# A shorter warm-up matmul, TensorE's tail transposes and expert counts at other places, the root table earlier, two endings behind a branch

## The chip, the cores and the metric

The kernel runs on one core of a Trainium2 chip. The metric is the device time of one execution in microseconds (us); lower is better. TensorE (PE) multiplies, VectorE (DVE) and ScalarE (ACT) do the elementwise work, GpSimd (POOL) a little of it, and SyncE (SP) issues most of the transfers.

## The reference

One step of a decoder layer for 320 tokens (256 of a prompt, 64 of eight sequences) of width 1024: a mixer, then a mixture of 32 experts, then a last norm.

```python
h = rmsnorm(x, norm_mix_w); proj = h @ w_in            # 1024 x 3584
y_conv = bg * short_conv(cg * v_c, ...)                # 512 channels
o, new_hgrn = hgrn2_chunked(q, logf, k, i, state)      # 4 heads, 128 x 128 states
x = x + concat(y_conv, norm(o) * gnorm_w * silu(g)) @ w_out
t = rmsnorm(x, norm_ffn_w)
vals, idx = top_k(t @ router_w + router_b, 4); gates = softmax(vals)
for e in range(32):                                    # w_*[e]: 1024 x 1024 float32
    a = minimum(t @ w_gate[e] + b_gate[e], 7); u = clip(t @ w_up[e] + b_up[e], -7, 7)
    y += combine[:, e] * (((u + 1) * a * sigmoid(1.702 * a)) @ w_down[e] + b_down[e])
y_out = rmsnorm(x + y, final_norm_w)                   # and the new states
```

The 96 expert matrices are 4 MiB each, 403 MB together, and each is read once.

## The kernel before

**Phases.** The input projection and the HGRN2 levels run first (to about 157 us of the trace), then the output projection `wout` with the router beside it (to about 197 us), then the first expert's tokens are gathered and the 32 experts run one after the other.

**An expert.** At most 64 tokens (slots) go to an expert in a round. TensorE gathers their rows from three bf16 parts of the normed rows (`gather`, L1535 and L1538), turns the last expert's hidden rows and this one's tokens (`turn_hidden` L1697, `turn` L1625), turns the selection (`turn_gates`, L1600, L1609), and then does the last expert's down product, this one's gate product, the scatter of the last expert's result (L1639) and the up product. Each product is `product`, 16 float32 matmuls in the code of L1679, which the trace shows as 32 (x32), behind two short ones for the bias (L1654). An expert thus takes three products, and its down product stands in the next expert's turn.

**Loops.** Experts 0 and 1 are written out. The other 30 are a hardware loop (`pe.Fori(0, LOOPS)`, L1734) of six passes with five experts each; the other engines have the same loop. A pass of TensorE's loop is 1627 instructions: 550 matmuls in the code, which are 790 weight loads and 790 matmuls in the engine's stream, and 47 waits, register instructions and the branch. In that stream a bf16 matmul or a transpose is two instructions and a float32 product's matmul is four. Counted in the built program, 3228 instructions of TensorE stand before the loop's first one.

**Weights.** SP issues each matrix as one 4 MiB transfer into a ring of five places. Matrix i is issued when product i-5 has read its place (`wUsed`). The matrices at both ends come in halves and quarters, so that a product can begin with a part. They are numbered 3e for gate, 3e+1 for up, 3e+2 for down; number 93 is the gate matrix of expert 31.

**Further rounds.** `further_rounds` (L311 to L326) reads the number of rounds and branches. With one round, as here, each engine runs `ending` in the branch's first part and then jumps over the code of the further rounds; that code is long on TensorE (some 2300 instructions).

**Start and end.** Before the inputs are there, TensorE runs nine matmuls of 512 columns on a constant tile (`keep_busy`, L1244). `tails` (L1419) are four transposes of the last convolution rows, which ACT copies out (L668) and sends. `counts` (L1500) are three matmuls that count the tokens of each expert. At the end ACT scales the last down product (`yLast`, L759), loads the table of the square root (L651), and `norms` squares the three blocks (L769); for the third block TensorE's `fold_final` adds two halves (L1255), from which ACT's root, DVE's reciprocal and product and the last transfers follow. SP's `outputs` sends the results.

Of the kernel before, what the change touches and what calls it, by code (L numbers as in the profile page):

```python
# [5 lines left out]
def hybrid_shortconv_hgrn2_moe_step(nc, A):  # L6
# [91 lines left out]
    LG_BANK, PART_BANK = 5, 6  # L98
    POS_BANK, COUNT_AT = [5, 5, 6], 384
# [10 lines left out]
    with ctx:  # L110
# [48 lines left out]
        tailT = view(R1, 3328, shape=(512,))  # L159
# [94 lines left out]
        h2Parts, roundsDone, epsOut, maskOut = (sem("h2_parts"), sem("rounds_done"), sem("eps_out"),  # L254
# [4 lines left out]
        finScale, fnwIn, ptLastOut = sem("fin_scale"), sem("fnw_in"), sem("pt_last_out")  # L259
        x2Kept, accSet, combDone = sem("x2_kept"), sem("acc_set"), sem("comb_done")  # L260
# [5 lines left out]
        busyOut = sem("busy_out")  # L266
# [68 lines left out]
        def _(sp):  # L335
# [140 lines left out]
            further_rounds(sp, all_loads, ending=outputs)  # L476
# [47 lines left out]
        def _(act):  # L524
# [3 lines left out]
            act.wait_ge(epsOut, 1)  # L528
# [101 lines left out]
            def root2(b):  # L630
                if b < 2:
                    act.wait_ge(ssq2Done, b + 1)
                    total = st[:, 9 + b:10 + b]
                else:
                    act.wait_ge(foldMM, 2)
                    total = ps[:, PART_BANK, 0:1]
                act.activation(st[:, 12 + b:13 + b], total, ACT.Sqrt, bias=epsT[:], scale=1.0 / D).then_inc(root2Done, 1)
# [46 lines left out]
            root2(2)  # L684
            def one_round(r):
# [71 lines left out]
                act.activation(PTLast[:], slots_of(E - 1), ACT.Copy).then_inc(ptLastOut, 1)  # L757
                act.wait_ge(wUsed, (r + 1) * (LPE * E) + START)
# [3 lines left out]
            def norms():  # L762

                bring_table(ACT.Sqrt, 3)
# [26 lines left out]
        def _(dve):  # L791
# [14 lines left out]
            did(dve.memset(epsT[:], EPS), epsOut)  # L806
            dve.memset(busy, 1.0).then_inc(busyOut, 1)
# [178 lines left out]
            X2T_BANK = [6, 7]  # L986
# [35 lines left out]
            def remainder(b, p):  # L1022

                hf = h2f[:, b % 2, 0:WIDE[b]]
                dve.wait_ge(partDone, 2 * b + 1 + p)
                if p == 0:
                    dve.wait_ge(normed, b + 1)
                    TT(hf, hf, h2p[0][b], ALU.subtract).then_inc(resid, 1)
                else:
                    dve.wait_ge(resid, b + 1)  # L1030
                    if b:
                        dve.wait_ge(tailOut, 32)
                    TT(h2p[2][b], hf, h2p[1][b], ALU.subtract).then_inc(h2Parts, 1)

            def choose(b):

                dve.wait_ge(lgMM, b + 1)
                need(did(STT(lg[:, b, :], ps[:, LG_BANK, E * b:E * b + E], st[:, 15 + b:16 + b], rb[:], ALU.mult, ALU.add)))
# [19 lines left out]
            def place(b):  # L1058
# [3 lines left out]
                need(did(STT(posm[:, b, 0:E], ps[:, POS_BANK[b], 128 + E * b:128 + E * b + E], 1.0, sel[:, b, :], ALU.add, ALU.mult), posOut))  # L1062
# [51 lines left out]
            def one_round(r):  # L1114
# [59 lines left out]
                if isinstance(r, int):  # L1174
                    gate_parts(slice(0, 1)).then_inc(combDone, 1)
                    dve.wait_ge(roundsDone, 1)
                    rounds.append(count_of_rounds(dve))
# [60 lines left out]
        def _(pe):  # L1238
# [7 lines left out]
            pe.wait_ge(busyOut, 1)  # L1246
            keep_busy(9)
# [189 lines left out]
            def turn_x2(b):  # L1437
                if b == 2:
                    pe.wait_ge(x2TOut, 2)
                    for half in range(2):  # L1440
                        pe.wait_ge(x2Done, 3 + half)
                        for c in range(2 * half, 2 * half + 2):
                            ins = TR(ps[:, 6 + half, 128 * c:128 * c + 128], xb[2][:, 128 * c:128 * c + 128], ident)
# [20 lines left out]
            def sum_logits(b):  # L1464
# [3 lines left out]
                pe.wait_ge(*((selDone, b) if b else (tailTOut, 1)))  # L1468
                MM(ps[:, LG_BANK, E * b:E * b + E], lgPart, fours[:], start=True, stop=True).then_inc(lgMM, 1)

            def logits(half):
# [3 lines left out]
                pe.wait_ge(posOut, 2)  # L1475
# [6 lines left out]
            def positions(b):  # L1482
# [5 lines left out]
                for at in range(0, 128, n):  # L1488
                    ins = MM(ps[at:at + n, POS_BANK[b], 128 + E * b:128 + E * b + E], trib[0:n, 0:n], sel[0:n, b, :], start=(b == 0), stop=True)
                ins.then_inc(posMM, 1)  # L1490

            def earlier_blocks(b):

                for a in range(b):
                    MM(ps[:, POS_BANK[b], 128 + E * b:128 + E * b + E], onesb[:], sel[:, a, :], start=(a == 0), stop=False)

            def counts():

                for a, (_, na) in enumerate(TOK):
# [48 lines left out]
            tails()  # L1548
# [26 lines left out]
            counts()  # L1575
# [3 lines left out]
            def one_round(r):  # L1579
# [14 lines left out]
                def turn_gates(e, m):  # L1594
# [3 lines left out]
                    pe.wait_ge(uDone, e + START)  # L1598
                    for b, (t0, n) in enumerate(TOK):
# [163 lines left out]
            further_rounds(pe, one_round, close_round, ending=fold_final)  # L1763
# [44 lines left out]
```

## Time and profile before

| | us |
|---|---|
| median of 3 runs | 1145.14 |
| lowest, highest | 1144.82, 1148.22 |
| profiled execution, its own time | 1145.91 |
| its span, first to last instruction | 1144.1 |
| TensorE busy | 1098.0 (96%) |
| VectorE busy | 285.6 (25%) |
| ScalarE busy | 174.4 (15%) |
| mean granted TensorE clock | 0.98 |
| read from HBM | 428.26 MB, 378 GB/s over the span with what is written |

How to read the rows further down: in the chain of waits each row is a start, a length and what the chain ran through; "issue" is time for which the profile shows no cause. A time of a view counts from the start of the span. "PEldq" is the sequencer that feeds TensorE, "SPq" that of SyncE; a branch that it takes has a duration there. A row of the transfers' view gives the line, how many were issued in the window, their size, and the median time from issue to landing.

### The profile page before, as it was taken

The page shows a single profiled execution, that of the slowest core. Times are in us where ns is not written, and L with a number is a line of the kernel's source. Part 1 is how long each engine was busy: PE and PEld are TensorE (multiplying, and loading weights), DVE is VectorE, ACT ScalarE, POOL GpSimd, SP SyncE. Part 2 cuts the span into 40 slices and gives each one's busy share as a digit, 9 for nine tenths or more (in the row PEclk, how much of TensorE's full clock was granted, in tenths as well). Part 3 has the DMA queues.
Part 4 walks back from the last instruction along what each step waited for, and adds up shares of the span by engine and source line. Part 5 has one row for each costly group of instructions (what it writes and reads, how often), then busy time and mean ns, then how long its engine had stood idle before and what let it go on. Part 6 is the DMA issues. An engine that isn't in the chain of part 4 may idle for free.

```text
span 1144.1 us, 15330 instructions
## 1 busy us (share of the span) xinstructions
PE 1098.0 (96%) x6369; PEld 465.1 (41%) x6370; DVE 285.6 (25%) x609; ACT 174.4 (15%) x354; POOL 18.2 (2%) x45
## 2 busy tenths in 40 slices
PE   8999999999999799998999989999899999899996
PEld 5667754433333333333333323333333333333332
DVE  3165464411222111111222111222111111122211
ACT  4100124211111011111111101111111111111112
POOL 0002000000000000000000000000000000000000
PEclk9999999999999899999999998999989999899999
DMA  9971259999999999999999999999999999999961
GB/s 321 333 217 45 103 199 396 377 426 434 414 432 432 428 409 432 432 428 432 416 434 428 432 432 417 435 427 434 426 420 428 434 431 428 423 428 427 426 277 48
DMA packets 43076, 433.17 MB, mean 379 GB/s; under 512 B 3999, under 2 KB 23251, under 8 KB 26869
## 3 DMA queue, kind: packets, MB, share of 16 engines
q1 hardware_dynamic: 42112, 431.03, 90.8%
q8 instruction: 66, 1.08, 0.4%
q10 hardware_dynamic: 885, 0.95, 0.2%
q14 instruction: 13, 0.11, 0.0%
HBM read 428.26 MB, written 3.71 MB: 378 GB/s over the span
## 4 chain that ended last, share of the span: by engine, by line
PE 94%; issue 3%; DMA 1%; DVE 1%; ACT 1%; ACTq 0%; DVEq 0%
PE ps L1679 58%; PE ps L1306 9%; PE ps L1639 6%; PE ps L1535 4%; PE ps L1431 3%; PE ps L1654 3%; PE ps L1538 2%; PE ps L1625 2%; PE ps L1697 2%; PE ps L1296 1%; PE ps L1600 1%; PE ps L1609 1%; DMA ring<-in_w_in 1%; PE ps L1334 0%; DMA x<-in_x_prompt 0%
## 5 line engine op out<-in xcount | busy, mean ns | idle before, releaser
L1679 PE MATMUL ps<-ring,RT 128*64 128x512 f32 x2040 | 448.6, 592 | 0.0
L1679 PEld LDWEIGHTS ps<-ring,RT 128*64 128x64 f32 x2040 | 144.0, 137 | 271.4 <-issue 265.7
L1679 PE MATMUL ps<-ring,R 128*64 128x512 f32 x1024 | 229.4, 601 | 0.0
L1679 PEld LDWEIGHTS ps<-ring,R 128*64 128x64 f32 x1024 | 73.1, 140 | 135.8 <-issue 133.7
L1306 PE MATMUL ps<-R,ring 128*128 128x320 f32 x384 | 107.4, 436 | 0.8 <-DMA ring<-in_w_in 0.8
L1306 PEld LDWEIGHTS ps<-R,ring 128*128 128x128 f32 x384 | 71.7, 190 | 32.2 <-issue 2.7
L1191 DVE TENSOR_SCALAR RT<-ps 128x512 f32<-128x512 f32 x32 | 22.1, 692 | 227.3 <-PE ps L1679 227.3
L1141 DVE SCALAR_TENSOR_TENSOR RT<-ps,R 128x512 f32<-128x512 f32 x31 | 23.3, 751 | 220.7 <-ACT R L720 220.7
L693 ACT ACTIVATE RT<-ps 128x512 f32<-128x512 f32 x31 | 18.5, 597 | 345.4 <-PE ps L1538 345.4
L1639 PE MATMUL ps<-R 64*128 64x512 bf16 x558 | 69.3, 380 | 0.0
L1535 PE MATMUL ps<-R,P 128*64 128x512 bf16 x372 | 50.7, 409 | 13.0 <-issue 13.0
L1182 DVE TENSOR_SCALAR RT<-ps 128x512 f32<-128x512 f32 x32 | 22.1, 692 | 131.3 <-PE ps L1679 130.6
L720 ACT ACTIVATE R<-ps,R 128x512 bf16<-128x512 f32 x31 | 21.3, 687 | 208.1 <-PE ps L1679 208.1
L710 ACT ACTIVATE RT<-RT 128x512 f32<-128x512 f32 x32 | 20.2, 630 | 179.2 <-DVE RT L1182 179.2
L1132 DVE TENSOR_TENSOR RT<-ps,par 128x512 f32<-128x512 f32 x31 | 21.4, 692 | 100.9 <-PE ps L1625 100.9
L1639 PEld LDWEIGHTS ps<-R 64*128 64x128 bf16 x558 | 23.3, 98 | 56.3 <-issue 38.3
L1538 PE MATMUL ps<-R,P 128*64 128x256 bf16 x372 | 30.8, 288 | 15.1 <-issue 15.1
L1535 PEld LDWEIGHTS ps<-R,P 128*64 128x64 bf16 x372 | 22.2, 112 | 47.5 <-issue 34.8
L1654 PE MATMUL ps<-R,eh 128*64 128x512 bf16 x192 | 40.1, 414 | 0.9 <-ACT R L715 0.7
L1538 PEld LDWEIGHTS ps<-R,P 128*64 128x64 bf16 x372 | 23.3, 113 | 25.2 <-issue 18.6
L1185 DVE TENSOR_TENSOR RT<-RT 128x512 f32<-128x512 f32 x32 | 22.2, 693 | 24.5 <-ACT RT L710 24.5
L1625 PE MATMUL ps<-consts,RT 128*128 128x128 f32 x128 | 25.8, 329 | 1.4 <-ACT RT L693 0.5
(254 smaller groups left out, 603.0 us busy)
## 6 DMA issues: line engine op xcount, KB each, us to landing
ring<-in_w_up SPq DMA_DIRECT2D x25, 4096.0 KB, 17.6
ring<-in_w_down SPq DMA_DIRECT2D x25, 4096.0 KB, 20.2
ring<-in_w_gate SPq DMA_DIRECT2D x24, 4096.0 KB, 20.5
ring<-in_w_up SPq DMA_DIRECT2D x12, 2048.0 KB, 14.9
ring<-in_w_gate SPq DMA_DIRECT2D x12, 2048.0 KB, 18.1
ring<-in_w_down SPq DMA_DIRECT2D x10, 2048.0 KB, 16.3
ring<-in_w_in SPq DMA_DIRECT2D x14, 1024.0 KB, 11.9
ring<-in_w_down SPq DMA_DIRECT2D x8, 1024.0 KB, 16.6
```

What stands on the lines that cost most here:

```text
L1141: STT(yrest, ps[:, DOWN_BANK, :], gsl[:, buf(j):buf(j) + 1], ysb[0], ALU.mult, ALU.subtract).then_inc(yRest, 1)
L1182: TS(ga, ps[:, GATE_BANK, :], LIMIT, None, ALU.min).then_inc(aDone, 1)
L1185: TT(gt, ga, gs, ALU.mult).then_inc(tDone, 1)
L1306: ins = MM(ps[:, n % 2, 0:NT], slot_k(L, 256)[:, k, 128 * half:128 * half + 128], hT[:, k, :], start=(k == 0), stop=(k == KT - 1))
L1431: ins = MM(dst, mixT[k][:, t0:t0 + n], w[:, 512 * half:512 * half + 512], start=(k == 0), stop=(k == KT - 1))
L1535: ins = MM(in_fours(to), P[:, b, 0:SLOTS], half_of(h2p[part][b], half), start=(b == 0 and part == 0), stop=False)
L1538: ins = MM(in_fours(to[:, 256 * at:256 * at + 256]), P[:, 2 + at, 0:SLOTS], half_of(h2p[part][2], half), start=False, stop=(part == 2 and ...
L1625: ins = TR(ps[:, to, 128 * c:128 * c + 128], fourth(xgs, c), ident)
L1639: ins = MM(acc_rows(b, half), slots_of(j)[64 * half:64 * half + 64, t0:t0 + n], ysb[part][64 * half:64 * half + 64, :], start=False, stop= ...
L1654: MM(shape(ps[64 * half:64 * half + 64, to, :]), eh[:, par, :], cols(bias3[:, mat, :], half), start=True, stop=False)
L1679: ins = MM(shape(ps[64 * half:64 * half + 64, to, :]), lhs(k), cols(w, half), start=False, stop=(n == KT - 1))
L1697: ins = TR(ps[:, DOWN_BANK, 128 * c:128 * c + 128], fourth(hid, c), ident)
```

## The change

It does these things, and nothing else:

- The nine warm-up matmuls become 43 of 32 columns and 5 of 512 columns; the two signals `epsOut` and `busyOut` become one, `fillOut`.
- `tails` stands behind the whole of `wout` instead of after its first block, writes another bank (6 instead of 5), and ACT copies and sends it after the third block's root instead of after the first's, from another place in memory. DVE's wait for that transfer moves behind the counting of rounds. The transposed third block goes to banks 5 and 7 instead of 6 and 7, with waits that fit.
- `counts` stands in the first expert's `turn_gates` instead of ahead of `gather_first(1)`.
- ACT loads the square root's table ahead of its wait for the last down product instead of after `yLast`.
- SP's `outputs` and TensorE's `fold_final` are no longer written in both parts of the branch but once, behind it. ACT's and DVE's endings stay in it.

By count, 3309 instructions of TensorE stand before its loop: 39 more matmuls of two instructions and three more waits, 81 in all. The loop itself keeps its 1627.

```diff
@@ further_rounds of SP and of TensorE
-            further_rounds(sp, all_loads, ending=outputs)
+            further_rounds(sp, all_loads)
+            outputs()
...
-            further_rounds(pe, one_round, close_round, ending=fold_final)
+            further_rounds(pe, one_round, close_round)
+            fold_final()
@@ ACT
             root2(0)
-            act.wait_ge(tailMM, 1)
-            act.activation(tailT[0:18, :], ps[0:18, LG_BANK, :], ACT.Copy).then_inc(tailTOut, 1)
             keep_x2(0)
-            act.wait_ge(tailTOut, 1)
-            act.dma_start(A["new_conv_prompt"][0, 0], tailT[0:2, :]).then_inc(tailOut, 16)
-            act.dma_start(A["new_conv_sample"][0].rearrange("b w c -> (b w) c"), tailT[2:18, :]).then_inc(tailOut, 16)
...
             root2(2)
+            act.wait_ge(tailMM, 1)
+            act.activation(tailT[0:18, :], ps[0:18, TAIL_BANK, :], ACT.Copy).then_inc(tailTOut, 1)
+            act.wait_ge(tailTOut, 1)
+            act.dma_start(A["new_conv_prompt"][0, 0], tailT[0:2, :]).then_inc(tailOut, 16)
+            act.dma_start(A["new_conv_sample"][0].rearrange("b w c -> (b w) c"), tailT[2:18, :]).then_inc(tailOut, 16)
...
                 act.activation(PTLast[:], slots_of(E - 1), ACT.Copy).then_inc(ptLastOut, 1)
+                bring_table(ACT.Sqrt, 3)
                 act.wait_ge(wUsed, (r + 1) * (LPE * E) + START)
                 act.activation(yLast, ps[:, DOWN_BANK, :], ACT.Copy, scale=gsl[:, buf(E - 1):buf(E - 1) + 1]).then_inc(yHigh, 1)
...
             def norms():
 
-                bring_table(ACT.Sqrt, 3)
@@ TensorE
-            pe.wait_ge(busyOut, 1)
-            keep_busy(9)
+            def keep_busy_in_bits(n):
+
+                for _ in range(n):
+                    MM(ps[0:32, 1, 0:32], busy[:, 0:32], busy[:, 0:32], start=True, stop=True)
+
+            pe.wait_ge(fillOut, 2)
+            keep_busy_in_bits(43)
+            keep_busy(5)
...
             def tails():
                 pe.wait_ge(tailIn, 1)
+                pe.wait_ge(lgPartOut, 2)
                 for c in range(4):
-                    ins = TR(ps[0:18, LG_BANK, 128 * c:128 * c + 128], tail[:, c, :], ident)
+                    ins = TR(ps[0:18, TAIL_BANK, 128 * c:128 * c + 128], tail[:, c, :], ident)
...
             def counts():
 
+                pe.wait_ge(posOut, 3)
...
             pe.wait_ge(stSOut, NH)
-            tails()
             wout(1, range(KT // 2))
...
             wout(2, range(7, KT))
+            tails()
             turn_x2(2)
             logits(0)
             pe.wait_ge(ssq2Done, 3)
-            sum_halves(st[:, 11:12], ps[:, PART_BANK, 0:1]).then_inc(foldMM, 1)
+            pe.wait_ge(x2TOut, 4)
+            sum_halves(st[:, 11:12], ps[:, FOLD_BANK, 0:1]).then_inc(foldMM, 1)
             logits(1)
             pe.wait_ge(earlyP, 1)
             pe.wait_ge(h2Parts, 2)
+            pe.wait_ge(root2Done, 3)
             gather_first(0)
-            pe.wait_ge(root2Done, 3)
+            pe.wait_ge(lgRead, 3)
             earlier_blocks(2)
             positions(2)
-            counts()
             gather_first(1)
...
                     pe.wait_ge(uDone, e + START)
+                    if isinstance(r, int) and e is e0:
+                        counts()
```

TensorE at the very start of the program, with the change (the warm-up and what follows it):

```order
L1249 MATMUL ps<-RT 32x32 x43
L1244 MATMUL ps<-RT 128x512 x5
L1256 MATMUL ps<-consts,parRows 128x52
L1267 MATMUL ps<-consts,R 128x128 x8
L1261 MATMUL ps<-st,fold 64x1 x2
```

Before, one row of nine matmuls (L1244, 128x512 x9) stood ahead of the transpose of `parRows`; 48 matmuls stand there now.

TensorE from the last piece of `wout` (128x512 product, L1431) to the first expert's first transposes, before:

```order
L1431 MATMUL ps<-ring 64x512 x2
L1443 MATMUL ps<-consts,x 128x128 x4
L1478 MATMUL ps<-rw,R1 64x32 x8
L1255 MATMUL ps<-st,fold 64x1 x2
L1478 MATMUL ps<-rw,R1 64x32 x8
L1514 MATMUL ps<-R1,P 64x256 x12
L1495 MATMUL ps<-sel,onesb 128x32 x2
L1489 MATMUL ps<-sel,trib 64x32 x2
L1500 MATMUL ps<-sel,onesb 128x32 x3
L1514 MATMUL ps<-R1,P 64x256 x12
L1522 MATMUL ps<-x,R1 64x256 x4
L1600 MATMUL ps<-identb,P 128x128 x2
```

The same place with the change (lines are some eight to twelve higher):

```order
L1438 MATMUL ps<-ring 64x512 x2
L1426 MATMUL ps<-consts,tail 18x128 x4
L1451 MATMUL ps<-consts,x 128x128 x4
L1486 MATMUL ps<-rw,R1 64x32 x8
L1261 MATMUL ps<-st,fold 64x1 x2
L1486 MATMUL ps<-rw,R1 64x32 x8
L1523 MATMUL ps<-R1,P 64x256 x12
L1503 MATMUL ps<-sel,onesb 128x32 x2
L1497 MATMUL ps<-sel,trib 64x32 x2
L1523 MATMUL ps<-R1,P 64x256 x12
L1531 MATMUL ps<-x,R1 64x256 x4
L1509 MATMUL ps<-sel,onesb 128x32 x3
```

The four tail transposes now stand between `wout` and the third block's transposes, and the three counting matmuls behind the gathers.

TensorE's end in the program, with the change (before, `fold_final`'s two matmuls, L1255, stood between the last two rows):

```order
L1691 MATMUL ps<-ring,R1 64x512 x16
L1756 MATMUL ps<-RT,PTLast 128x512 x4
L1756 MATMUL ps<-RT,PTLast 64x512 x2
L311 TENSOR_LOAD rounds
L311 ISA x2
L316 COMPARE_AND_BRANCH
L316 UNCONDITIONAL_BRANCH
```

The jump over the further rounds (the last row) came after `fold_final` and comes ahead of it now.

## Rows read from the trace of the kernel before

**Rows 1.** Chain of waits, around the loop's second return: start us, us, what

```profile
525.59 6.87 PE ps L1679 x32
532.46 2.96 issue
535.41 2.54 PE ps L1535 x12
538.75 2.38 issue
561.98 6.87 PE ps L1679 x32
589.64 6.87 PE ps L1679 x32
```

**Rows 2.** Who waited for whom, TensorE: total us, times, longest us

```profile
PE ps L1538 <- issue: 15.1, 5, 4.5
PE ps L1535 <- issue: 13.0, 5, 3.0
```

**Rows 3.** Branches of TensorE's sequencer: count, ns min/median/max, when

```profile
L1734 PEldq COMPARE_BRANCH  x6: 83/6552/6927, 380.7 to 1117.1; - x6
L1734 PEldq COMPARE_BRANCH  x1: 6927/6927/6927, 528.1 to 528.1; - x1
L316 PEldq COMPARE_BRANCH  x2: 87/2386/4686, 1133.6 to 1137.7; - x2
```

**Rows 4.** Instruction queue: packets, MB, share; the page, 532 to 548 us, 541.2 to 673 us

```profile
q8 instruction: 66, 1.08, 0.4%
...
q8 instruction: 3, 0.05, 1.3%
...
q8 instruction: 6, 0.10, 0.3%
```

**Rows 5.** Stretches: us, PE, PEld, DVE, ACT, POOL busy (x), clock, DMA share, GB/s

```profile
400.00:410.00 10.00, 10.00 (x50) 3.30 (x48) 1.44 (x2) 1.32 (x2) 0.00 (x0) 1.00 0.93 372
535.40:538.75 3.35, 3.34 (x18) 1.76 (x18) 0.00 (x0) 0.00 (x0) 0.00 (x0) 0.55 1.06 455
562.00:679.00 117.00, 116.92 (x664) 44.31 (x660) 22.83 (x44) 14.93 (x32) 0.95 (x4) 1.00 1.00 430
```

**Rows 6.** Transfers, matrix 93: SP's issues, then second half's landing time, then its product

```profile
1062.82 3.76 SPq L348 DMA_DIRECT2D ring<-in_w_gate  x2
...
ring<-in_w_gate SPq DMA_DIRECT2D x1, 2048.0 KB, 21.8
...
1105.08 7.03 PE L1679 MATMUL ps<-ring,RT 128*64 128x512 f32 x32
```

**Rows 7.** Chain of waits, 160 to 206 us

```profile
170.82 0.44 PE ps L1419 x4
...
196.62 0.43 DVE x L993
...
200.57 0.27 PE ps L1500 x3
```

**Rows 8.** Timeline of the end: start, us, engine, line, what

```profile
1132.69 2.99 PE L1744 MATMUL ps<-RT,PTLast 64*128 64x512 f32 x12 [0.88 <-ACT RT L759]
1132.81 1.28 ACT L651 ACT_TABLE_LOAD   x1 [0.26 <-issue]
...
1134.21 1.01 ACT L769 ACTIVATE R<-ps 128x1024 f32<-128x1024 f32 x1
...
1137.68 0.28 PE L1255 MATMUL ps<-st,fold 128*64 128x1 f32 x4 [2.00 <-ACT R L769]
...
1139.50 0.56 ACTq L778 DMA_DIRECT2D y_sample<-R  x1
```

**Rows 9.** Timeline of the start

```profile
1.94 4.02 PE L1244 MATMUL ps<-RT 128*128 128x512 bf16 x9 [1.94 <-DVE RT L807]
...
6.31 0.34 PE L1250 MATMUL ps<-consts,parRows 52*128 52x52 f32 x1 [0.34 <-DMA consts<-in_consts]
```

More of the change, by code:

```diff
@@ L97, in hybrid_shortconv_hgrn2_moe_step @@
     UP_BANK, GATE_BANK, DOWN_BANK = 5, 6, 7
-    LG_BANK, PART_BANK = 5, 6
-    POS_BANK, COUNT_AT = [5, 5, 6], 384
+    LG_BANK, PART_BANK, TAIL_BANK, FOLD_BANK = 5, 6, 6, 7
+    POS_BANK, COUNT_AT = 5, 384
     FIRST_BANK = (4, 7)
@@ L158, in hybrid_shortconv_hgrn2_moe_step @@
         stP = view(RT, 0, "p (h d) -> p h d", shape=(4, 128), h=4)
-        tailT = view(R1, 3328, shape=(512,))
+        tailT = view(RT, 512, shape=(512,))
         x2T = view(R1, 3840, "p (k t) -> p k t", shape=(8, 128), k=8)
@@ L259, in hybrid_shortconv_hgrn2_moe_step @@
         finScale, fnwIn, ptLastOut = sem("fin_scale"), sem("fnw_in"), sem("pt_last_out")
+        lgRead = sem("lg_read")
         x2Kept, accSet, combDone = sem("x2_kept"), sem("acc_set"), sem("comb_done")
@@ L805, in _ @@
             TT, TS, STT = dve.tensor_tensor, dve.tensor_scalar, dve.scalar_tensor_tensor
-            did(dve.memset(epsT[:], EPS), epsOut)
-            dve.memset(busy, 1.0).then_inc(busyOut, 1)
+            did(dve.memset(epsT[:], EPS), fillOut)
+            dve.memset(busy, 1.0).then_inc(fillOut, 1)
             did(dve.memset(u[:, :, 0:2], 0.0))
@@ L985, in _ @@
             WB = [0, 2, 4]
-            X2T_BANK = [6, 7]
+            X2T_BANK = [5, 7]
             def add_mixer(b):
@@ L1037, in choose @@
                 dve.wait_ge(lgMM, b + 1)
-                need(did(STT(lg[:, b, :], ps[:, LG_BANK, E * b:E * b + E], st[:, 15 + b:16 + b], rb[:], ALU.mult, ALU.add)))
+                need(did(STT(lg[:, b, :], ps[:, LG_BANK, E * b:E * b + E], st[:, 15 + b:16 + b], rb[:], ALU.mult, ALU.add), lgRead))
                 need(did(dve.max(mx[:, b, :], lg[:, b, :])))
@@ L1061, in place @@
                 dve.wait_ge(selDone, b + 1)
-                need(did(STT(posm[:, b, 0:E], ps[:, POS_BANK[b], 128 + E * b:128 + E * b + E], 1.0, sel[:, b, :], ALU.add, ALU.mult), posOut))
+                need(did(STT(posm[:, b, 0:E], ps[:, POS_BANK, 128 + E * b:128 + E * b + E], 1.0, sel[:, b, :], ALU.add, ALU.mult), posOut))
                 if b == 2:
@@ L1175, in one_round @@
                     gate_parts(slice(0, 1)).then_inc(combDone, 1)
+                    dve.wait_ge(tailOut, 32)
                     dve.wait_ge(roundsDone, 1)
@@ L1439, in turn_x2 @@
                     pe.wait_ge(x2TOut, 2)
+                    pe.wait_ge(posOut, 2)
                     for half in range(2):
@@ L1442, in turn_x2 @@
                         for c in range(2 * half, 2 * half + 2):
-                            ins = TR(ps[:, 6 + half, 128 * c:128 * c + 128], xb[2][:, 128 * c:128 * c + 128], ident)
+                            ins = TR(ps[:, 5 + 2 * half, 128 * c:128 * c + 128], xb[2][:, 128 * c:128 * c + 128], ident)
                         ins.then_inc(x2TMM, 1)
@@ L1467, in sum_logits @@
                 pe.wait_ge(foldOut, 2)
-                pe.wait_ge(*((selDone, b) if b else (tailTOut, 1)))
+                if b:
+                    pe.wait_ge(selDone, b)
                 MM(ps[:, LG_BANK, E * b:E * b + E], lgPart, fours[:], start=True, stop=True).then_inc(lgMM, 1)
@@ L1474, in logits @@
                 pe.wait_ge(rwOut, 1)
-                pe.wait_ge(posOut, 2)
                 for k in ((0, 1, 4, 5), (2, 3, 6, 7))[half]:
@@ L1488, in positions @@
                 for at in range(0, 128, n):
-                    ins = MM(ps[at:at + n, POS_BANK[b], 128 + E * b:128 + E * b + E], trib[0:n, 0:n], sel[0:n, b, :], start=(b == 0), stop=True)
+                    ins = MM(ps[at:at + n, POS_BANK, 128 + E * b:128 + E * b + E], trib[0:n, 0:n], sel[0:n, b, :], start=(b == 0), stop=True)
                 ins.then_inc(posMM, 1)
@@ L1494, in earlier_blocks @@
                 for a in range(b):
-                    MM(ps[:, POS_BANK[b], 128 + E * b:128 + E * b + E], onesb[:], sel[:, a, :], start=(a == 0), stop=False)
+                    MM(ps[:, POS_BANK, 128 + E * b:128 + E * b + E], onesb[:], sel[:, a, :], start=(a == 0), stop=False)
             def counts():
+                pe.wait_ge(posOut, 3)
                 for a, (_, na) in enumerate(TOK):
```

9 lines of the change are left out of this document (3 added, 6 removed).

## The prediction

> **What bounds the kernel now.** I read the chain of waits first: it is TensorE nearly throughout, so I looked for the time in which TensorE does nothing. Within the loop an expert takes 27.66 us, from one up product to the next (561.98 to 589.64, [rows 1]). Across the loop's return the same stretch takes 36.39 us (525.59 to 561.98). So this return costs 8.73 us beyond the work, and there are five returns.
>
> Where these go: TensorE stops twice, 2.96 us right at the return and 2.38 us after the first 18 matmuls of the new pass [rows 1]. "Issue" means that no other engine and no weight transfer is behind it. Both gaps come once per return: 13.0 and 15.1 us over five, 28.1 together, or 5.6 each [rows 2]. The other 3.1 us of this return are work at half clock: the granted clock is 0.55 of full between the gaps [rows 5], a mixture of the 2.4 and 1.2 GHz levels, and the first 12 matmuls of 535.41 take 2.54 us. In the steady stretch it is 1.00.
>
> The cause is in the sequencer. The loop's branch takes 0.08 us where it falls through and up to 6.93 us where it is taken [rows 3]. In the 16 us around the return three packets of 16 KB come on the instruction queue, and only six in the next 132 us [rows 4]. Code comes in pieces. In the steady stretch 1324 weight loads and matmuls take 117 us [rows 5] and a piece is used up in about 132 / 6 = 22 us [rows 4], so a piece holds about 249 of them, which with the waits and register instructions among them (47 in 1627) makes 256. One piece lands after the jump. It holds only the first 36 weight loads and matmuls (18 matmuls) with their waits, some 40 instructions, and then TensorE waits again, for the next piece. So a piece's edge lies about 40 instructions behind the loop's first one.
>
> The second limit is not in TensorE's rows. The transfer engines are busy 1.00 of the steady stretch and move 430 GB/s [rows 5]. An expert's three matrices are 12.58 MB: 29.2 us at that rate, longer than the 27.66 us that TensorE needs. With the returns, five experts take TensorE 5 x 27.66 + 8.7 = 147 us, against 146 us for their weights. Today the two limits stand side by side.
>
> **The loop's code, 81 instructions later.** The edge that was 40 behind the loop's first instruction comes to lie 41 ahead of it, and the next is 256 - 41 = 215 behind it. This does three things.
> - The second gap goes. A piece of 215 instructions lasts some 15 us, and a fetch took about 2.5 us where it was waited for. Even if it were only asked for at the edge, the sequencer runs ahead of TensorE: it reached the branch at 528.1 [rows 3], 4.3 us before the product ended at 532.46 [rows 1], so at most some 0.5 us would show.
> - The jump gets shorter. Today the branch is 1627 - 40 - 6 x 256 = 51 instructions behind an edge, so, as I read it, the piece that comes after the loop has just been asked for, and the jump's own fetch waits for it: 6.93 us. The jump at the program's end, with nothing under way, takes 4.69 us [rows 3]. With the change the branch stands 132 instructions (some 11 us) behind an edge, and I take 4.69 us. Less the 4.3 us that the sequencer is ahead, and some 0.35 us to restart, the gap is 0.7 us.
> - With gaps of 0.7 us I expect the clock to stay at 2.4 GHz, as in the steady stretch.
>
> A return then costs 0.7 to 1.5 us instead of 8.7; I take 0.7, and TensorE alone would gain 5 x 8.0 = 40 us.
>
> The Trainium skill (Runtime: NRT & Kernel Launch, Instruction fetch mechanics) says that code comes in 16 KiB blocks of 256 instructions with the next block fetched ahead, and that a taken branch outside the window waits for a fetch; by that the trace agrees. The same section gives TensorE room for 2048 instructions. By that the loop of 1627 would stay inside and the shift would gain nothing. The six and three packets per pass [rows 4] speak against it.
>
> **What the weights let through.** 40 us is more than the weights allow. Their transfers run without a pause, so a faster TensorE doesn't bring them earlier. The closest place near the end is the gate matrix of expert 31 (number 93). Its second half is issued at about 1066.2, lands 21.8 us later at 1088.0, and is needed by the fifth of eight k-tiles of a product that starts at 1105.1, so at 1108.5 [rows 6]: 20.5 us of room, 20.3 with a semaphore's time. All that follows it on TensorE (23 us) stays as it is. TensorE will then wait for weights for the other 18 to 20 us, spread over the later experts.
>
> What brings the transfers themselves earlier counts too. After the first return no matrix had been issued for long, and 372 GB/s instead of 430 flow for 10 us [rows 5]: 58 / 430 x 10 = 1.3 us, of which I take 1.0 (0 to 1.5). The other part is the next paragraph's 0.5.
>
> The Trainium skill (DMA: Bandwidth & Descriptors, Specifications) states a fabric ceiling of 435 GB/s, by which an expert can't take less than 28.9 us; the 430 of the trace agrees.
>
> **Tails and counts.** The four tail transposes are 0.44 us of the chain at 170.82 [rows 7]. They move to where TensorE waits for DVE's first half of the third block anyway (0.43 us from 196.62, and 0.14 us to start), which hides them but for 0 to 0.2 us. ACT's copy and two issues go to its idle time after the third root. The counts are 0.27 us at 200.57 [rows 7]; the gather behind them waits for DVE's index tile, so 0.1 to 0.2 are won, and at their new place TensorE waits for the copies of the gathered rows. Together 0.5 us won (0.2 to 0.7). Full cover gone, it would be 0.3 us lost.
>
> **The warm-up.** Nine matmuls took 4.02 us and ended 0.35 us before they had to [rows 9]. Five take some 2.2 us. 43 small ones are not in this trace. By the wide ones' 4.02 / 9 = 0.45 us as the upper bound they would be absurdly long at 19 us; the nearest rows are the counts, 0.27 / 3 = 0.09 us each [rows 7] for 32 columns, and by them 43 take at most 3.9 us, at best half. So TensorE is ready at 6.1 to 8.1. I take 0 us of loss (0 to 1.2), since by the lower end nothing waits.
>
> **The end.** ACT's table (1.28 us) no longer stands between `yLast` and the first square. But that square needs the first scatters: four of twelve matmuls that start at 1132.69 [rows 8], done at about 1133.8. It started at 1134.21, so the squares come 0.3 us earlier, no more. The jump over the further rounds is now ahead of `fold_final`. The branch is read at 1133.6, and the jump takes 4.69 us [rows 3]: TensorE can fold at 1138.5 at the earliest, where it did so at 1137.68 [rows 8]. The chain from there is unchanged (ACT's root, DVE, the send at 1139.50, the end at 1144.1). Net 0.8 us lost (0 to 1.2). SP's jump is hidden: it has sent its last weights 20 us before.
>
> **The sum.** Span 1144.1 - 20.3 - 1.0 - 0.5 + 0.8 = 1123.1. The profiled execution took 1145.91, 1.8 more than its span, and the runs' median is 0.8 below that: 1124.1 us. A measurement of this kernel can tell about 0.3% (3.4 us) from no change.
>
> **The rivals.**
> - *TensorE's gain gets through whole*, because the transfers run faster once more of them are queued: 1144.1 - 40 - 1.5 + 0.8 and so about 1104 us. Against it: the rate is the same with few and with many queued, but for [rows 5]'s first stretch. 4%.
> - *Only part of the gaps goes*, for instance the second gap with the clock still falling at the first (3 us won per return, 15 in all): 1129 us, up to 1138 if it is only some of the returns. If just the jump stays at 6.9 us and all else goes, 5.3 us per return or 26 are won, and the weights cut it to the same 1124. 13%.
> - *The place in the code doesn't matter*, and jump and second fetch cost what they cost (the Trainium skill's 2048 instructions would mean this too, with another cause for the gaps): only the small parts are left, 1145 us (1143 to 1147). 8%.
> - *Slower:* the piece behind a jump is fetched only when its predecessor is empty, and the sequencer is not ahead there, since the transposes' waits hold it. Then the jump costs 4.7 + 2.5 us as now, and the new edge, 215 instructions in, stops a product for 4.7 us. A return would cost the first gap's 3.0, these 4.7 and at least today's 3.1 of half clock [rows 1], 10.8 instead of 8.7 us, and the kernel takes 1145 + 5 x 2.1 = 1156 us. It decides from the point where a return costs over 8.7 us. 5%.
>
> **How the numbers follow.** My case, weights as the limit, has 70%, and its own bounds are 1120 to 1128 us: the tails, warm-up and end make +-1.5, the pauses in the transfers (which come at other times in every run) +-2. The range that leaves out two in ten reaches into the second rival: 1119 to 1132. Faster by over 0.3%: 70 + 4 + 13 = 87%; within: 8%; slower: 5%.
>
> **What would show it.** In the changed kernel's profile: branches of the loop at 4.7 us instead of 6.9, one packet less per pass on the instruction queue, no gap 18 matmuls into a pass, clock 1.00 through the loop, and in the later passes waits of TensorE for the weights' transfers, which there are none of now, 18 to 20 us together. The last product ends at about 1110, and the fold comes 0.8 us later relative to it. I am wrong if TensorE's gaps at the returns stay over 2 us, or if the transfers move clearly more or less than 430 GB/s.

## The result and the profile after

The changed kernel takes 1116.24 us (median of 4 runs, 1115.36 to 1117.82) against 1144.98 us (1143.85 to 1148.22) of the kernel before, run beside it: 0.9746 times, 95% interval 0.9723 to 0.9769, and so 28.7 us faster. The forecast of 1124.1 had the direction and the limit right and the size too small; 1116.2 lies outside its range of 1119 to 1132.

The page of the changed kernel: TensorE's row, clock and rate in 40 slices, the queues, the chain that ended last by engine.

```profile
span 1114.2 us, 15412 instructions
PE 1086.0 (97%) x6408; PEld 459.9 (41%) x6409; DVE 285.6 (26%) x609; ACT 174.4 (16%) x354; POOL 18.1 (2%) x45
...
PEclk9999999999999999999999999999999999999999
...
GB/s 319 333 243 9 144 159 382 385 407 433 416 431 431 431 433 432 431 433 432 429 432 431 432 433 431 432 433 432 432 433 433 432 432 433 432 422 429 428 424 231
...
q8 instruction: 21, 0.34, 0.1%
...
PE 75%; DMA 22%; DVE 1%; ACT 1%; issue 0%; SPq 0%; ACTq 0%; DVEq 0%
```

Three things to see. The instruction queue (q8, which brings code) has 21 packets where it had 66 [rows 4]. "Issue" (time for which the profile shows no cause) has left the chain, and 22% of it are now transfers. From the tenth slice to the 35th the rate is 429 to 433 GB/s but for one slice of 416, without the lower slices of before.

The chain of waits around the second return of the loop (start us, us, what), and the branches of TensorE's sequencer (ns min/median/max):

```profile
516.37 6.87 PE ps L1691 x32
523.24 1.35 PE ps L1544 x12
...
544.16 6.87 PE ps L1691 x32
```

```profile
L1746 PEldq COMPARE_BRANCH  x6: 83/215/250, 380.5 to 1089.1; - x6
L1746 PEldq COMPARE_BRANCH  x1: 220/220/220, 518.9 to 518.9; - x1
```

The up product that stood 36.39 us ahead of the next pass's first one [rows 1] now stands 544.16 - 516.37 = 27.79 us ahead of it, 0.13 more than in a stretch without a return (27.66). The branch taken at 518.9 lasts 0.22 us where it lasted 6.93 [rows 3]. Both gaps are gone [rows 2], not just the second.

The instruction queue in the last 24 us of the first pass, to the first return (one packet); between 390 and 1100 us the transfers' view has no row of this queue at all:

```profile
q8 instruction: 1, 0.02, 0.3%
```

Stretches of the changed kernel as in [rows 5] (clock, DMA share and GB/s at the end), then matrix 93 as in [rows 6]: the two issues, the second half's time to landing, the waits of TensorE, and the product.

```profile
400.00:410.00 10.00, 10.00 (x58) 3.28 (x56) 1.38 (x2) 0.63 (x1) 0.24 (x1) 1.00 0.99 426
562.00:679.00 117.00, 116.77 (x664) 44.47 (x662) 24.28 (x46) 16.17 (x34) 0.94 (x4) 1.00 1.00 432
```

```profile
1030.60 3.76 SPq L348 DMA_DIRECT2D ring<-in_w_gate  x2
...
ring<-in_w_gate SPq DMA_DIRECT2D x1, 2048.0 KB, 45.2
...
PEld ps L1691 <- DMA ring<-in_w_gate: 18.8, 14, 2.0
PE ps L1691 <- DMA ring<-in_w_gate: 9.8, 11, 1.2
...
1079.26 3.65 PE L1691 MATMUL ps<-ring,RT 128*64 128x512 f32 x16 [1.17 <-DMA ring<-in_w_gate]
```

Weights are the limit: the second half of matrix 93 is issued at 1034.03, 32 us earlier than before, lands 45.2 us later at 1079.2, and the second half of its product waits for it. Before, it landed at 1088.04. So the transfers themselves became earlier by 8.8 us. That is the part for which the prediction had only 1.0 us.

The end (start us, us, engine, line), against [rows 8]:

```profile
1102.67 0.69 ACT L761 ACTIVATE RT<-ps,R 128x512 f32<-128x512 f32 x1 [5.50 <-PE ps L1691]
1104.67 1.02 ACT L770 ACTIVATE R<-ps 128x1024 f32<-128x1024 f32 x1 [1.31 <-PE ps L1756]
1107.82 0.19 ACT L770 ACTIVATION_READ_ACCUMULATOR R<-ps 128x1 f32 x1
1108.48 0.26 ACT L777 ACTIVATE st<-ps,epsT 128x1 f32<-128x1 f32 x1 [0.46 <-PE ps L1261]
1109.98 0.56 ACTq L779 DMA_DIRECT2D y_sample<-R  x1
```

### The profile page after: what moved, and what is told of

Its sections match the earlier page's. It is cut to its first block, busy times and chain, and to the rows that moved or that the text cites. A ratio compares the mean times of both kernels' runs of the same rounds, so it can differ in the third digit from the quotient of the medians.

```text
span 1114.2 us, 15412 instructions
## 1 busy us (share of the span) xinstructions
PE 1086.0 (97%) x6408; PEld 459.9 (41%) x6409; DVE 285.6 (26%) x609; ACT 174.4 (16%) x354; POOL 18.1 (2%) x45
## 4 chain that ended last, share of the span: by engine, by line
PE 75%; DMA 22%; DVE 1%; ACT 1%; issue 0%; SPq 0%; ACTq 0%; DVEq 0%
PE ps L1691 44%; DMA ring<-in_w_up 18%; PE ps L1312 10%; DMA ring<-in_w_gate 4%; PE ps L1651 4%; PE ps L1438 3%; PE ps L1544 3%; PE ps L1666 2%; PE ps L1637 2%; PE ps L1547 1%; PE ps L1302 1%; PE ps L1709 1%; PE ps L1612 1%; PE ps L1621 1%; DMA x<-in_x_sample 0%
## 5 line engine op out<-in xcount | busy, mean ns | idle before, releaser
L1691 PE MATMUL ps<-ring,R 128*64 128x512 f32 x1024 | 225.1, 592 | 0.0
L1544 PE MATMUL ps<-R,P 128*64 128x512 bf16 x372 | 47.2, 387 | 0.0
L1544 PEld LDWEIGHTS ps<-R,P 128*64 128x64 bf16 x372 | 21.3, 109 | 32.5 <-issue 18.6
L1438 PE MATMUL ps<-ring 128*128 128x512 f32 (+1 forms) x72 | 27.1, 598 | 0.0
L1143 DVE TENSOR_TENSOR R<-RT,R 128x512 bf16<-128x512 f32 x31 | 21.5, 692 | 21.6 <-ACT R L723 21.6
L1547 PE MATMUL ps<-R,P 128*64 128x256 bf16 x372 | 26.2, 274 | 0.0
## 6 DMA issues: line engine op xcount, KB each, us to landing
ring<-in_w_down SPq DMA_DIRECT2D x10, 2048.0 KB, 40.8
```

The lines of the kernel that those rows point to most:

```text
L1438: ins = MM(dst, mixT[k][:, t0:t0 + n], w[:, 512 * half:512 * half + 512], start=(k == 0), stop=(k == KT - 1))
L1544: ins = MM(in_fours(to), P[:, b, 0:SLOTS], half_of(h2p[part][b], half), start=(b == 0 and part == 0), stop=False)
L1547: ins = MM(in_fours(to[:, 256 * at:256 * at + 256]), P[:, 2 + at, 0:SLOTS], half_of(h2p[part][2], half), start=False, stop=(part == 2 and ...
L1691: ins = MM(shape(ps[64 * half:64 * half + 64, to, :]), lhs(k), cols(w, half), start=False, stop=(n == KT - 1))
```

## Experiments

The question after the result was double: why does the loop no longer fetch code at all, and why did the weights come 8.8 us earlier? The first six runs set a theory R (room: TensorE keeps eight pieces of 256 instructions, and a loop that fits in with the piece fetched ahead is not fetched again) against P (the prediction's: every pass is fetched again), S (the gain is in the small parts) and G (a gradual effect of the shift). The next two set F (the code's fetches delay the weights) against D (the depth of SP's queue does).

### One part alone, and all but that part

`e1_warmup_only`, on the kernel before:

```diff
-            keep_busy(9)
+            keep_busy_in_bits(43)
+            keep_busy(5)
```

> The kernel before with the warm-up alone changed (43 small and 5 wide matmuls for 9 wide ones): the loop's code lies 78 instructions later and nothing else moves. Theory R (room for 2048 instructions, 8 pieces of 256: the loop's 1627 stay in it when they and the piece fetched ahead touch no more than 8 pieces): the first instruction is then 39 behind an edge, the loop stays in, some 21 packets on the instruction queue instead of 66, the loop's branch 0.2 us, and of the gain of 28.7 us all but a few tenths is here: 1116 to 1118 us. Theory P (the prediction's: each pass fetches its code again, the shift only shortens the jump to 4.7 us and removes the second gap): 61 packets, branch 4.7 us, and about the same time as the changed kernel. Theory S (the gain is mostly in the moved tails, counts, table and outputs): 1140 us or more.

Measured: 1116.73 us (0.9755, 0.9738 to 0.9772), 21 packets. `e2_no_shift` is the changed kernel with the same lines the other way round:

```diff
-            keep_busy_in_bits(43)
-            keep_busy(5)
+            keep_busy(9)
```

> The changed kernel with nine wide warm-up matmuls as before and no small ones: tails, counts, table and outputs stay moved, the loop's code lies 3 instructions later than before instead of 81. R and P: the edge is 36 behind the loop's first instruction, the loop runs as before, 66 packets on the instruction queue and branches of 6.9 us, 1143 to 1145 us. S: 1116 to 1120.

Measured: 1143.51 us (1.0000, 0.9988 to 1.0011), 66 packets, branches up to 6.9 us. The whole gain is in the warm-up's line, and the next runs show that it is the place of the code. Tails, counts, table and endings together are worth 0 within 1.3 us.

### The edge, from both sides

The warm-up's small matmuls shift the loop by two instructions each. `e3_20_bits` and `e4_24_bits` differ in four of them:

```diff
-            keep_busy_in_bits(43)
+            keep_busy_in_bits(20)      # and 24
```

> The changed kernel with 20 small matmuls instead of 43: the shift is 35 instructions, and the loop's first instruction lies 4 ahead of an edge. R: loop and piece ahead touch 9 pieces, so every piece is fetched again in every pass: about 66 packets on the instruction queue and 1140 to 1146 us. P: the jump's piece holds 4 instructions, then the next one is waited for; the branch stands 87 behind an edge, so jump 4.7 us and second gap some 2.5 us: about 1124 to 1130 us. Theory G (a gradual effect of the shift): a time about in the middle, 1132 us.

> The changed kernel with 24 small matmuls instead of 43: the shift is 43 instructions, 8 more than in the kernel with 20, and the loop's first instruction lies 4 behind the same edge. R: seven pieces and the one ahead, the loop stays in: 21 packets, branch 0.2 us, 1116 us as the changed kernel. P: 1116 to 1124 too, but with 61 packets and branches of 4.7 us. G: about 1130 us.

Measured: 1153.22 us with 20 (1.0089, 1.0067 to 1.0110) and 1116.73 us with 24 (0.9760, 0.9743 to 0.9777): eight instructions are worth 36 us. Branches, first with 20, then with 24, and TensorE's waits with 20:

```profile
L1746 PEldq COMPARE_BRANCH  x6: 83/6652/7106, 379.7 to 1122.5; - x6
```

```profile
L1746 PEldq COMPARE_BRANCH  x6: 83/215/254, 380.3 to 1089.2; - x6
```

```profile
PE ps L1544 <- issue: 42.3, 5, 8.8
```

With 20 the two gaps of a return have become one of up to 8.8 us, since, by the prediction's edge, the piece that comes after the jump holds only four or five of the loop's instructions. That is the picture of pieces which the prediction had. What it didn't have is the kernel with 24, in which nothing is fetched. The number of 1153 was 7 us above R's range.

The far end of the loop is tried with `e5_103_bits` and `e6_107_bits` (the same line with 103 and 107).

> The changed kernel with 103 small matmuls instead of 43: the shift is 201 instructions, the loop's first instruction lies 162 behind an edge and its last 4 ahead of one, so the loop touches seven pieces. R (the loop stays in the room when it and the piece ahead are 8): about 21 to 22 packets on the instruction queue, branch 0.2 us, 1116 us plus what the longer warm-up costs (60 x 31 ns = 1.9 us later, so 1117 to 1118). If the shift rather helps by distance from the old place or by any place behind the old edge, the same.

> The changed kernel with 107 small matmuls instead of 43: the shift is 209 instructions, the loop's first instruction lies 170 behind an edge and its last 4 behind one, so the loop touches eight pieces and with the one ahead nine. R: every piece is fetched again in every pass, 66 packets, 1143 us or more, though the shift is 8 instructions longer than in the kernel with 103. A theory in which only the place of the loop's first instruction counts (few instructions between it and the next edge are what hurts): 86 instructions to the edge are plenty, 1118 to 1124 us.

Measured: 1115.42 us with 103 (0.9743, 0.9700 to 0.9786; 22 packets, branch 0.2 us), 1125.16 us with 107 (0.9835, 0.9791 to 0.9878; 67 packets). R had 1117 to 1118 for the one with 103, and the longer warm-up that it reckoned with doesn't show. With 107, branches, the waits, and the page's queue:

```profile
L1746 PEldq COMPARE_BRANCH  x6: 83/6420/6526, 379.9 to 1095.7; - x6
```

```profile
PE ps L1544 <- issue: 12.3, 5, 2.6
PE ps L1666 <- issue: 3.0, 4, 1.5
```

```profile
q8 instruction: 67, 1.10, 0.4%
```

With an edge 40 instructions behind the old place of the loop, as the prediction had it, the kernels with 24 and 103 touch seven pieces, those with 20 and 107 eight. Seven stay in, eight do not, at either end. R had the packets right and the time too high by 18 us; the rival by the place of the loop's first instruction (1118 to 1124) had the time nearly right and said nothing of the packets. Both effects are there: the count of pieces decides whether code is fetched again, and some 86 instructions between the jump and the next edge keep the second gap away when it is.

`e6_107_bits` is the state that the prediction described, with code fetched in every pass and the second gap nearly gone (3.0 us over four returns). What a return costs there is read from the chain, from one up product to the next across it:

```profile
662.00 6.87 PE ps L1691 x32
668.87 2.58 issue
...
694.12 6.87 PE ps L1691 x32
```

That is 32.12 us, 4.46 more than the 27.66 of a stretch without a return. The five returns cost 3.7 to 5.1 us each, 21.8 us together, where the same reading gives 45.3 us for the kernel before and 0.7 us for `e9_after_light_weights` further down. The prediction had 0.7 us for each return of this state. That 1125 us agrees with its 1124 all the same is because the 23.5 us which TensorE gains are just about what the weights let through: all waits for weights together lengthen this kernel by some 2 us. It is nearer to the prediction's rival in which the jump alone stays at 6.9 us (26 us won, and the same 1124).

### Why the weights come earlier

In all kernels with whole matrices two neighbouring landings of 4 MiB lie 9.71 us apart, except where one comes 0.1 to 1.7 us late (2.9 once in `e3_20_bits`). From matrix 12 on these delays add up to 10.8 us in the kernel before and to 1.5 us in the changed one. With the fetches, the depth of SP's queue changed too: a matrix of before lands 13 to 26 us after its issue, one of after up to 45. `e7_short_queue` undoes the depth and leaves the code in, and `e8_fetches_and_deep_queue` does the reverse.

```diff
@@ e7_short_queue, SP, on the changed kernel
-                used = lambda n: 4 * (i - NG_) + n + START
+                used = lambda n: 4 * (i - NG_) + n + START + min(9, max(0, (i - 24) // 4))
@@ e8_fetches_and_deep_queue, TensorE's scatter, on e2_no_shift
-                             ins = MM(acc_rows(b, half), ..., ysb[part][64 * half:64 * half + 64, :], ...)
+                             ins = MM(acc_rows(b, half)[:, 0:64], ..., ysb[part][64 * half:64 * half + 64, 0:64], ...)
```

> The changed kernel with SP's loads of the later matrices issued up to 9 quarter products (20 us) later, so that at no time more than about two matrices are queued: issue to landing stays at about 20 us instead of growing to 41. No code is fetched in the loop. Theory F (the pauses of the weights' stream were the code's fetches): the matrices go on landing every 9.71 us, last landing as in the changed kernel (1098 to 1100), 1116 to 1117 us. Theory D (the pauses went because more loads are queued): pauses of 0.5 to 1.5 us come back, 8 us in all, 1124 us.

> The kernel with the loop 3 instructions later than before (every piece fetched again, 66 packets) and with the scatter's matmuls over 64 of 512 columns, so that TensorE has some 3 us less work per expert; this leaves out most of the sum over the experts. TensorE then gains about 16 us per pass, more than the 8.7 us that a return costs, and the loads queue up as in the changed kernel (issue to landing over 30 us) while the code is still fetched. F: the weights' stream keeps its pauses, 8 to 10 us in all from matrix 12 on, last landing at 1106 to 1108, and 1121 to 1125 us. D: no pauses, last landing at 1099, 1115 to 1117 us.

Measured: 1116.82 us with the short queue (0.9750, 0.9706 to 0.9794), 1122.72 us with fetches and the deep queue (0.9807, 0.9762 to 0.9853). For each, in this order, the stretch from 390 to 970 us with its DMA share and GB/s, and from the transfers' view of it the instruction queue (where it has a row) and the gate matrices' median time to landing:

```profile
390.00:970.00 580.00, 570.83 (x3238) 216.33 (x3234) 116.58 (x225) 76.14 (x163) 4.96 (x21) 1.00 1.00 432
...
ring<-in_w_gate SPq DMA_DIRECT2D x19, 4096.0 KB, 19.3
```

```profile
390.00:970.00 580.00, 534.73 (x3162) 209.11 (x3160) 114.23 (x220) 74.64 (x160) 4.75 (x20) 0.98 1.00 430
...
q8 instruction: 37, 0.61, 0.4%
...
ring<-in_w_gate SPq DMA_DIRECT2D x19, 4096.0 KB, 41.2
```

In the short queue the matrices land 19.3 us after issue, about as before (20.5), and from 390 to 970 us none is late. The 2.7 us of delay in all lie in the main in the first pass (1.4 us at 329), and the last matrix lands at 1099.4, as in the changed kernel. With fetches the queue is as deep as in the changed kernel (41.2), and 10.1 us of delay are back, the last one lands at 1106.6. Each of its six larger delays (1.5 us each) has a packet of the instruction queue between the landing ahead and the late one. D has fallen: the code's fetches delay the weights, 45 of them by 8 to 9 us, about 0.2 us each, though many a fetch delays nothing and some delay 1.5 us. Which ones was not found out.

One delay of the kernel before is of the other kind, though, the one that the prediction saw. Behind the first return the transfer engines are not full, and the matrix that lands there is 1.2 us late:

```profile
404.00:409.00 5.00, 5.00 (x28) 1.69 (x26) 1.44 (x2) 1.32 (x2) 0.00 (x0) 1.00 0.88 328
```

In the six stretches of `e8_fetches_and_deep_queue` that hold its larger delays the share is 0.98 to 1.00.

### What TensorE alone would take

`e9_after_light_weights` and `e10_before_light_weights` bring matrices 12 to 83 only to three quarters:

```diff
-                sp.dma_start(ring[:, at:at + 4, :]..., w_exp[m][e])
+                sp.dma_start(ring[:, at:at + 3, :]..., w_exp[m][e, :, 0:6 * D])   # i >= 12
```

> The changed kernel with matrices 12 to 83 brought only to three quarters (the last two of eight k-tiles are multiplied with what an earlier matrix left there, so the experts' sums are wrong from there on). It asks what TensorE alone would take. Theory R (returns now cost 0.15 us instead of 8.7): all 5 x 8.6 = 43 us come through, no waits for weights in the loop, 1144.1 - 43 and so a span of about 1101, 1103 us. Theory W (something else than weights, ACT's or DVE's work on an expert, would stop TensorE next): 1108 us or more, with its waits named by another engine.

> The kernel before with the same lighter weights (matrices 12 to 83 to three quarters, part of the computation left out in the same way). If TensorE with its returns was the limit before, and the transfers' pauses cost nothing there, it takes 1143 to 1146 us as before. If the pauses or the transfers already held it up, it gains 3 us or more. The code fetches now meet free transfer engines: if a taken branch and the second gap are as long as before (6.5 us, 2.4 us and more), the weights' traffic doesn't lengthen the fetch; if they shrink to some 2 to 4 us, it does.

Measured, one run each: 1102.47 us and 1143.26 us. The chain by engine of the changed kernel so lightened, then branches and waits of the kernel before so lightened:

```profile
PE 97%; ACT 1%; DVE 1%; issue 0%; DMA 0%; ACTq 0%; SPq 0%; DVEq 0%
```

```profile
L1738 PEldq COMPARE_BRANCH  x6: 82/6154/7478, 380.9 to 1112.8; - x6
...
PE ps L1542 <- issue: 14.6, 5, 3.2
PE ps L1539 <- issue: 12.6, 5, 3.5
```

Before, a quarter less weights brings 1.7 us at most, and the one run lies within the 1141.89 to 1149.57 us of the kernel before beside it: TensorE and its returns were the limit, and the delays of the transfers cost nothing that could be told. The jumps and gaps are hardly shorter (6.15 against 6.55 us at the branch, 27.2 against 28.1 us in the gaps). That does not settle what the weights' traffic does to them. Over the whole stretch the transfer engines were a fifth free, but during the branches themselves their share was 0.90 to 0.97. This is the longest of them:

```profile
819.70:827.20 7.50, 4.38 (x22) 1.21 (x18) 1.38 (x2) 0.00 (x0) 0.00 (x0) 0.98 0.94 363
```

The trace's packets say more of where a branch's time goes. In the five taken branches of the kernel before, the code's packet starts 3.4 to 4.5 us after the branch's start, takes 1.0 to 1.1 us, and the branch ends 1.4 to 1.5 us later. At the jump over the further rounds, with all weights landed, these are 2.4, 1.0 and 1.4 us. So the packet and what follows it are the same with and without the weights' traffic, and the difference lies ahead of the packet. What fills that time isn't shown.

After, TensorE alone would take 1102.5. It would gain 40.8 us against `e10_before_light_weights`, whose returns cost 40.7, and the weights keep back some 14 of these (1116.2 - 1102.5).

### The fold behind the jump

`e11_fold_in_branch` takes the endings back, `e12_after_again` is the changed kernel on the same chip.

```diff
-            further_rounds(sp, all_loads)
-            outputs()
+            further_rounds(sp, all_loads, ending=outputs)
...
-            further_rounds(pe, one_round, close_round)
-            fold_final()
+            further_rounds(pe, one_round, close_round, ending=fold_final)
```

> The changed kernel with TensorE's fold and SP's outputs back inside the branch, ahead of the jump over the further rounds, as they were before. The prediction's step (the jump stands on the path of the fold) says 0.8 us less than the changed kernel. The trace of the changed kernel (jump done at 1107.93, ACT's last square at 1108.01, fold at 1108.16) says 0.0 to 0.1 us.

> The changed kernel itself once more, on the chip of the three others, to compare them with: 1116 to 1117 us, 21 packets on the instruction queue.

Measured: 1115.69 us (0.9732, 0.9708 to 0.9756; 1114.06 to 1116.41) and 1116.48 us (0.9744, 0.9722 to 0.9767; 1116.14 to 1116.87). ACT's last square and the fold, then the branch over the further rounds, in the second of these:

```profile
1107.72 0.19 ACT L770 ACTIVATION_READ_ACCUMULATOR R<-ps 128x1 f32 x1
1108.56 0.28 PE L1261 MATMUL ps<-st,fold 128*64 128x1 f32 x4 [2.17 <-ACT R L770]
```

```profile
L316 PEldq COMPARE_BRANCH  x2: 83/1986/3888, 1104.4 to 1104.5; - x2
```

Here the jump took 3.89 us, to 1108.4, and the fold came 0.65 us behind ACT's last square (1107.91); in the profile of the result it took 3.35 us and the fold came 0.15 behind it, as in the kernel with the fold in the branch (1107.11 to 1107.26). The jump thus costs 0 to 0.5 us. How long it takes goes with the fold's place: 4.69 to 4.76 us in the four executions in which the fold stands ahead of it (before, `e1_warmup_only`, `e10_before_light_weights`, `e11_fold_in_branch`), 3.30 to 3.89 us in the ten in which it follows the first branch at once. The medians differ by 0.8 us, but the runs of the two overlap, and the last product also ended 0.8 us earlier in that profile. A kernel that is surely faster than the changed one this is not.

## Why the prediction was right and wrong

**The two limits: right.** TensorE with its returns was the limit before, and the weights are the limit after. Both were said from [rows 1, 5], and the light weights show both. TensorE waits for weights in the later experts only, from 729 us on.

**The returns: the cause wrong, the size near it by luck.** TensorE alone was to gain 40 us, and with light weights it gained 40.8. But the prediction let every pass fetch its code again (one packet less per pass, branches of 4.7 us), and what happened is that the loop stayed in TensorE's room (no packet, 0.22 us). Where the code is fetched again and the second gap is gone, in `e6_107_bits`, TensorE gains 23.5 us and not 40: the branch stays at 6.1 to 6.5 us, and a return costs some 4.4 us instead of 0.7. The first step that failed is the reading of [rows 4]. Six and three packets per pass were taken to show that no 2048 instructions fit. They show only that this loop at this place doesn't: it touches eight pieces of 256, and with the piece fetched ahead that is nine. The Trainium skill (Runtime: NRT & Kernel Launch, Instruction fetch mechanics) gives TensorE 2048 instructions, and the runs agree with it: with 24 and 103 small matmuls seven pieces are touched and stay, with 20 and 107 eight are touched and all are fetched anew. The prediction had that rule in hand and set it against the shift, without counting the pieces that the loop touches, though it had the edges for it: 40 instructions ahead of the first edge, six pieces, and 51 behind the last are eight.

**The jump: wrong where it is fetched.** 4.7 us was given to a jump with nothing under way. With 20 small matmuls the branch is some 87 instructions behind an edge and still takes 6.65 us, with 107 it is 4 behind one and takes 6.42. The distance to the edge does not set it, so the 6.9 us are not the jump's fetch behind another one. Why a jump out of the loop's end is longer than the one over the further rounds (3.3 to 4.8 us) stays open. Nor was that one a measure of a jump as such: it is 0.8 to 1.5 us shorter as soon as the fold no longer stands ahead of it.

**The weights: right as the limit, the term too small.** Room at matrix 93 was 20.3 us and is fully used. "A faster TensorE doesn't bring them earlier" was the step that failed, and with it the forecast: 1.0 us was put down for pauses of the transfers, and it was 8.8 us at matrix 93 (1088.04 to 1079.2). The prediction looked at one pause, behind the first return ([rows 5], 372 GB/s), and gave it to a short queue, which fits that one (1.2 us). The other delays were spread over the whole loop and belonged to the fetches, which the prediction kept. TensorE's loss to waits for weights was put at 18 to 20 us and came to some 15 (the stretches from up product to up product, less 27.66 each). The two errors are one: with the fetches still there, its 1124 is what `e6_107_bits` takes (1125.16), where the last matrix lands at 1107.3 us, near the 1108.2 of before, though there, too, the cost of the returns was not the one forecast.

**Tails and counts: 0.5 us said.** From the end of the HGRN part to the first expert's product 0.55 us are won (the part ended 0.39 us later, the product came at 203.87 instead of 204.03). Right.

**The warm-up: 0 said, 0 to 1.2 allowed.** The small matmuls took 1.33 us for 43, 31 ns each, a third of the 0.09 us taken from the counts. The first product of `w_in` came at 12.84 in this profile, 12.08 before, but at 11.33 in `e1_warmup_only` with the same warm-up: from 8.4 to 11.8 us the granted clock was 0.50 in the one (1.2 GHz) and 1.00 in the other. In `e2_no_shift`, with the nine wide ones, it came at 10.97. A cost of the small ones can't be told from that spread.

**The end: wrong in sign.** 0.8 us lost was said. From `yLast` to the last send it takes 1109.98 - 1102.67 = 7.31 us instead of 7.64. The table brings 0.35 us (first square 2.00 us behind `yLast` instead of 2.35), as the prediction said with 0.3. The jump costs 0 to 0.5 instead of 1.2, because it took 3.35 to 3.89 us and not the 4.69 of [rows 3], which had the fold ahead of it.

**The sum, corrected:** 1144.1 - 20.3 - 8.8, less 0.35 for the table and 0.4 because the last send's way to the end of the span was shorter (1109.98 to 1114.2 against 1139.50 to 1144.1), gives 1114.2, the span. Start, tails and counts don't appear in it, since the weights decide.

## What to carry to other kernels

Where a loop's code is near the size of TensorE's room, count the pieces of 256 instructions that it touches, plus the one fetched ahead; a few instructions more ahead of the loop can save every fetch, and a few too many bring them all back, here 36 us for eight instructions. Code fetches cost twice: at the jump, and as delays of other transfers where these are the limit. When one limit gives way, look at every traffic that the edit takes off the next one before calling that one fixed.

## What the runs showed of the hardware

- TensorE's code room: 8 pieces of 256 instructions, the piece ahead among them. It couldn't be told apart from a room of seven and one beside it.
- A taken branch lasts 0.22 us within the room and 5.7 to 7.5 us at the loop's end outside it. The jump over the further rounds, outside too, took 3.3 to 3.9 us, or 4.7 to 4.8 with the fold ahead of it. In both the time varies ahead of the code's packet, which takes some 1 us and is followed by 1.3 to 1.6 us until the branch ends.
- 16 KB of code on a full set of transfer engines delay the stream of 4 MiB transfers by 0.2 us in the mean, in lumps of up to 1.7 us. The late landing behind the first return of the kernel before (1.2 us) is another thing: the transfer engines' share there was 0.88.
- A bf16 matmul of 128 rows over 32 columns (128x32) took 31 ns in a row of 43 at the start, with its weight load.
- The weights' stream ran at 432 GB/s, the same with 19 us (`e7_short_queue`) and with 38 us (the changed kernel) from issue to landing.
